# Attention scores from rounded operands: two single-pass products in place of one float32 product, in a two-layer kernel

## The reference, cut to what matters

```
# first layer: NSA (selected and window branch), MoBA
s = einsum(q, k) * scale
s = s - slope[h] * (t_query - t_key)          # ALiBi
p = softmax(where(t_key <= t_query, s, NEG)); o = p @ v
# NSA, compressed branch: 31 keys, each at the centre of a block
s = einsum(q, kc) * scale - slope[h] * (t_query - cmp_center)
# second layer: forgetting attention, c = cumsum(log_sigmoid(f)) per head
s = einsum(q, k) * scale + c[query] - c[key]
p = softmax(where(t_key <= t_query, s, NEG)); o = p @ v
```

## Time and profile before

| | |
|---|---|
| Median of 3 runs | 3514.24 us |
| The profiled execution | 3515.05 us, of which its span 3513.0 us |
| PE busy in the span | 3197.4 us (91%) |
| DVE busy | 2842.7 us (81%) |
| ACT busy | 1426.1 us (41%) |
| POOL busy | 732.3 us (21%) |
| Stage att1 | 201.6 to 383.3 us |
| Stage att2 | 1945.4 to about 2058 us |

### The profile page before, as it was taken

How to read it: one execution, slowest core, us unless ns; L and a number is a source line. 1 busy time by engine, 2 the same in 40 slices (tenths; PEclk the granted TensorE clock), 3 DMA queues, 4 the chain that set the end, 5 groups by cost and what they waited for, 6 DMA issues and landing times. The chain is left out here.

```text
span 3513.0 us, 38582 instructions
## 1 busy us (share of the span) xinstructions
PE 3197.4 (91%) x13369; PEld 2158.7 (61%) x13369; DVE 2842.7 (81%) x4722; ACT 1426.1 (41%) x1756; POOL 732.3 (21%) x724
## 2 busy tenths in 40 slices
PE   7999979999999999999999999988788888888877
PEld 4878757777777777766787788544344433344432
DVE  5877679999999999967993554788888888888886
ACT  2235348888888888853233532111111111111110
POOL 0000021000000000010000100344444444444443
PEclk9999989999999999999999999999999999999999
DMA  7422279999999999973233024999999999999998
GB/s 284 163 85 103 75 253 390 407 406 404 406 405 403 407 407 403 410 275 117 96 99 117 25 85 168 403 420 421 421 414 416 408 414 410 421 419 403 421 419 345
DMA packets 251974, 1102.12 MB, mean 314 GB/s; under 512 B 21153, under 2 KB 30753, under 8 KB 185889
## 3 DMA queue, kind: packets, MB, share of 16 engines
q1 hardware_dynamic: 166397, 525.18, 39.3%
q0 software_dynamic: 79680, 558.14, 38.8%
q10 hardware_dynamic: 5760, 17.04, 1.2%
HBM read 1071.20 MB, written 33.03 MB: 314 GB/s over the span
## 5 line engine op out<-in xcount | busy, mean ns | idle before, releaser
L2061 DVE TENSOR_TENSOR moe_w_lo<-ring,moe_w_hi 128x2048 fp32r<-128x2048 f32 x384 | 860.6, 2282 | 25.1 <-ACT moe_w_hi L1909 24.0
L1909 ACT ACTIVATE moe_w_hi<-ring 128x2048 fp32r<-128x2048 f32 x380 | 720.7, 1915 | 153.4 <-DMA ring<-in_exp_w 138.4
L2850 PE MATMUL last_banks<-last_rows_b,ring 128*128 128x512 f32 x1024 | 502.5, 638 | 127.0 <-DVE ring L3050 126.7
L2850 PE MATMUL last_banks<-last_rows_a,ring 128*128 128x512 f32 x1024 | 478.4, 611 | 80.7 <-DVE ring L3050 80.4
L2942 ACT ACTIVATE last_gelu<-last_dot 128x2 f32<-128x2 f32 (+1 forms) x257 | 52.3, 203 | 1118.0 <-DVE last_dot L3047 1117.9
L2850 PEld LDWEIGHTS last_banks<-last_rows_b,ring 128*128 128x128 f32 x1024 | 197.8, 202 | 406.6 <-issue 209.5
L2850 PEld LDWEIGHTS last_banks<-last_rows_a,ring 128*128 128x128 f32 x1024 | 188.7, 193 | 324.9 <-issue 198.8
L2729 POOL DMA_INDIRECT last_rows_a<-in_peer_uv,last_ids x256 | 284.3, 1111 | 498.8 <-PE last_banks L2850 317.2
L2729 POOL DMA_INDIRECT last_rows_b<-in_peer_uv,last_ids x256 | 292.9, 1144 | 384.5 <-PE last_banks L2850 362.6
L3050 DVE TENSOR_SCALAR ring<-consts_sb,last_gelu,last_gates 128x128 f32<-128x128 f32 x512 | 161.8, 393 | 76.0 <-ACT last_gelu L2942 74.8
L1658 POOL COPY moe_col<-slots 128x1 uint32 (+1 forms) x30 | 34.8, 1159 | 856.4 <-PE moe_tp L1705 469.9
(11 more groups left out here) (583 smaller groups left out, 6334.3 us busy)
## 6 DMA issues: line engine op xcount, KB each, us to landing
ring<-in_exp_w SPq DMA_DIRECT2D x384, 1024.0 KB, 11.2
ring<-in_w_in SPq DMA_DIRECT2D x38, 1024.0 KB, 5.1
z<-in_ada_w SPq DMA_DIRECT2D x12, 1024.0 KB, 7.3
y_rows<-moe_y ACTq DMA_DIRECT2D x17, 512.0 KB, 6.8
ring<-in_ada_w SPq DMA_DIRECT2D x4, 2048.0 KB, 14.7
ring<-in_w_out SPq DMA_DIRECT2D x8, 1024.0 KB, 4.9
y_rows<-spare SPq DMA_DIRECT2D x1, 7680.0 KB
ring<-in_ada_w SPq DMA_DIRECT2D x4, 1024.0 KB, 9.7
```

What stands on the lines that cost most here:

```text
L1909: nc.scalar.activation(w_hi[:, slot, :], env.ring[:, slot, :], ACT.Copy).then_inc(hi_done, 1)
L2061: nc.vector.tensor_tensor(w_lo[:, slot, :], env.ring[:, slot, :], w_hi[:, slot, :].bitcast(F32), ALU.subtract).then_inc(lo_done, 1)
L2850: last = nc.tensor.matmul(sums(t)[:, q, :], diag[:, n % SL], slot(n)[:, D + q * W:D + (q + 1) * W], start=first, stop=final)
```

## The change

`score` works on rounded (F32R) operands. Four tiles take the place of `qt` and `kt`: `qa` holds the query's rounded value in its low 64 rows and the rest (query minus rounded query) in its high 64 rows; `ka` holds the rounded key twice; `kb` the rest of the key and one or two rows for the bias; `qb` the rounded query and the slope (or ones). The score is `qa` by `ka` over 128 rows, plus `qb` by `kb` over 65 or 66 rows, plus the mask as before. In the first layer the row of `kb` is the key's position, in the second it is minus c, rounded, and its rest. `cmp_score` multiplies `qa` in float32 by the compressed key stored twice, and its bias is now added on DVE.

```diff
             def operand(i, m):
 
-                n = base[i] + m
-                pe.wait_ge(prep, 2 * n + 2)
+                kind, u = heads[i].operands[m]
+                src, col = (zq, heads[i].q[u]) if kind == "q" else (zk, heads[i].k[u])
                 if i:
                     pe.wait_ge(tq_moved, first_move(i, m))
+                    pe.wait_ge(tq_rest, base[i] + m)
+                    pe.wait_ge(hi_twice, base[i] + m)
                 for t in range(NT):
-                    last = nc.tensor.transpose(turn_bank(i, m)[0:AUG, t * P:(t + 1) * P], rows[:, n % 4, t, :], ident)
+                    last = nc.tensor.transpose(turn_bank(i, m)[low, t * P:(t + 1) * P], src[:, t, col:col + HD], ident)
                 last.then_inc(tq_turn, 1)
...
                 i, t, u = step(g)
                 if t == 0:
                     pe.wait_ge(tq_moved, moves_before(i))
+                    pe.wait_ge(tq_rest, base[i] + len(heads[i].operands))
+                    pe.wait_ge(hi_twice, base[i] + len(heads[i].operands))
+                    if neg_c is not None:
+                        pe.wait_ge(aug_set, 1)
+                        pe.wait_ge(decay_landed[i % 2], 64 * (i // 2 + 1))
+                    else:
+                        pe.wait_ge(aug_set, 4 * NT)
+                        pe.wait_ge(aug_ok, queries(i, len(heads[i].q)))
                 end = (t + 1) * P
-                nc.tensor.matmul(sc[:, g % 2, 0:end], qt[0:AUG, q_place(i, u), t * P:end], kt[0:AUG, k_place(i, u), 0:end], start=True, stop=False)
+                nc.tensor.matmul(sc[:, g % 2, 0:end], qa[:, q_place(i, u), t * P:end], ka[:, k_place(i, u), 0:end], start=True, stop=False)
+                nc.tensor.matmul(sc[:, g % 2, 0:end], qb[0:HD + N_AUG, q_place(i, u), t * P:end], kb[0:HD + N_AUG, k_place(i, u), 0:end], start=False, stop=False)
                 nc.tensor.matmul(sc[:, g % 2, t * P:end], ident_b[:], causal_b[:], start=False, stop=True).then_inc(scored, 1)
...
             for g in range(STEPS):
                 i, n = g // UNITS, g % UNITS
+                if i + 1 < len(heads) and 2 <= n <= len(heads[i + 1].operands) + 1:
+                    operand(i + 1, n - 2)
                 turn(g)
...
-                if i + 1 < len(heads) and 1 <= n <= len(heads[i + 1].operands):
-                    operand(i + 1, n - 1)
...
                 act.wait_ge(tq_turn, first_move(i, m) + 1)
                 kind, u = heads[i].operands[m]
-                dst = qt[0:AUG, q_place(i, u)] if kind == "q" else kt[0:AUG, k_place(i, u)]
-                nc.scalar.activation(dst, turn_bank(i, m)[0:AUG, :], ACT.Copy).then_inc(tq_moved, 1)
-
+                dst = qa[low, q_place(i, u)] if kind == "q" else ka[low, k_place(i, u)]
+                nc.scalar.activation(dst, turn_bank(i, m)[low], ACT.Copy).then_inc(tq_moved, 1)
+                act.wait_ge(tq_moved, first_move(i, m) + 1)
+                twice = qb[low, q_place(i, u)] if kind == "q" else ka[high, k_place(i, u)]
+                nc.scalar.activation(twice, dst.bitcast(F32), ACT.Copy).then_inc(hi_twice, 1)
+
+            def move_act(g):
+
+                i, t, u = step(g)
+                act.wait_ge(turned, g + 1)
+                nc.scalar.activation(probt[:, g % 2, 0:(t + 1) * P], pt[:, g % 2, 0:(t + 1) * P], ACT.Copy).then_inc(moved_act, 1)
...
+            def rest(i, m):
+
+                kind, u = heads[i].operands[m]
+                dve.wait_ge(tq_moved, first_move(i, m) + 1)
+                if kind == "q":
+                    nc.vector.tensor_tensor(qa[high, q_place(i, u)], turn_bank(i, m)[low], qa[low, q_place(i, u)].bitcast(F32), ALU.subtract).then_inc(tq_rest, 1)
+                else:
+                    nc.vector.tensor_tensor(kb[low, k_place(i, u)], turn_bank(i, m)[low], ka[low, k_place(i, u)].bitcast(F32), ALU.subtract).then_inc(tq_rest, 1)
...
             for g in range(STEPS):
                 i, n = g // UNITS, g % UNITS
-                move(g)
+                if not by_act(g):
+                    move(g)
                 if g + 2 < STEPS:
                     maximum(g + 2)
+                if i + 1 < len(heads) and 2 <= n <= len(heads[i + 1].operands) + 1:
+                    rest(i + 1, n - 2)
...
+                pool.wait_ge(zero_set, 1)
+                for n in range(4):
+                    for t in range(NT):
+                        if n + t:
+                            pool.wait_ge(aug_set, NT * n + t)
+                        nc.gpsimd.tensor_scalar(kb[aug_rows, n, t * P:(t + 1) * P], env.const("iota")[aug_rows], float(t * P), None, ALU.add).then_inc(aug_set, 1)
...
-                    nc.gpsimd.tensor_copy(rows[:, n % 4, :, 0:HD], src[:, :, col:col + HD]).then_inc(prep, 1)
-                    nc.gpsimd.tensor_copy(rows[:, n % 4, :, HD:AUG], aug).then_inc(prep, 1)
+                        nc.gpsimd.tensor_scalar(qb[aug_rows, q_place(i, u), :], env.const("ones")[aug_rows, 0:1].to_broadcast([N_AUG, S]), head.slopes[u], None, ALU.mult
+                                                ).then_inc(aug_ok, 1)
...
+                sp.wait_ge(decay_hi, 1)
+                sp.wait_ge(decay_lo, 1)
+                for i, head in enumerate(heads):
+                    if i >= 2:
+                        sp.wait_ge(scored, UNITS * (i - 1))
+                    for u in range(2):
+                        for r in range(2):
+                            sp.dma_start(kb[HD + r:HD + r + 1, k_place(i, u), :].bitcast(F32), decay[head.decays[u]:head.decays[u] + 1, r, :].bitcast(F32)).then_inc(decay_landed[i % 2], 16)
```

155 lines of the change are left out of this document (96 added, 59 removed).

## The result

| | before | changed |
|---|---|---|
| three runs, us | 3513.53 to 3518.21 | 3659.35 to 3674.99 |
| median, us | 3514.24 | 3665.11 |
| profiled execution, us (span) | 3515.05 (3513.0) | 3674.99 (3673.2) |
| ratio to before, 95% interval | | 1.0421, 1.0404 to 1.0439 |

The forecast was 3545 with a range of 3521 to 3562. The direction was right; the cost is +151 us and not +30.

A forecast was written before the change was run, and what follows sets the result against it. PE, busy 13.22 of 13.22 us in a pair, was taken as the bound. The terms 25 + 1 + 0 - 2.5 + 4 + 2 = +29.5, rounded to +30 on 3515.05, gave 3545 us, range 3521 to 3562.

The forecast's parts named there:

- PE's gain: On PE in each attention head, two rounded passes per score put a pair's scores at 2.54 us, 1.84 less.
- The loop and its waits: From one operand's transposes to the next in a pair, 2.55 us; PE waits 4.1 us a head together.
- fourth wait: After a head's fourth operand, ACT's exponential stands behind rounding and second copy: 0.65 us more waiting on PE.
- 11 x 2.3: Eleven heads whose next head has four operands, each 2.3 us slower: +25 us, bounds +13 and +32.
- the NSA heads' 0: Six NSA heads before a head with one operand: 0 each, between -1.8 and +0.6; -11 to +4 in all.
- rival D: The clock falls: stage starts alone +3 us; heads a third of the time at 1.2 GHz, +20 and more, 3570; 5%.
- D's third: In the clock-falls case, attention heads running a third of the time at 1.2 GHz: +20 us and more.
- Last heads: Last head of each attention stage, with no operands to bring: -1.2 us each, -2.5 in all.
- Start of att1: First score waits for POOL's memset, 16 small instructions and one of 512: +4 us, bounds +2 and +8.
- Start of att2: First score waits for ACT's operand work and, beside it, four DMAs: +2 us, bounds +1 and +5.
- Everything else: Weight loads, zeros, later row DMAs, and memsets and copies in convolution and compressed keys: below 0.5 us.

The follow-up runs named there:

- e9: Changed kernel without rest and second copy (operand halves filled with ones), and ACT's exponential of the compressed scores one step later: 3528.4 us, ratio 1.0026.
- e2: Kernel before with float32 scores, plus the changed kernel's operand chain alone, its added results going to memory nobody reads: 3718.1 us, ratio 1.0558.
- e13: Changed kernel without the second copy on ACT (its halves filled with ones), the rest on DVE kept: 3654.2 us, ratio 1.0361.
- e1: Changed kernel with both rounded passes of each score issued twice, in both attention stages: 3624.0 us, ratio 1.0288.
- e12: Kernel before, unchanged, profiled once more: 3512.5 us.
- e11: Changed kernel with two banks, second copy on GpSimd, start on DVE, operands, rest and exponential reordered, third small ACT copy, NSA filler matmul: 3554.9 us, ratio 1.0095.
- e6: Changed kernel with two operand banks in att2 and the second copy on GpSimd: 3628.5 us, ratio 1.0318.
- e7: Changed kernel with att1's position row made by DVE in 4 instructions instead of 16 on GpSimd: median 3656.9 us, no ratio given.
- e8: Changed kernel with two banks where the head before has no compressed branch, second copy on GpSimd, att1's position row on DVE: 3598.0 us, ratio 1.0235.

## Why the prediction was wrong

Step by step, as the prediction put them:

- **PE's gain, 1.84 us a head.** Right. Without waits a pair takes 11.53 us (e9) against 13.22: 1.69. Beside the rounding of weight tiles it is 12.26 against 13.51: 1.25. The passes themselves are dearer than forecast (see below; a pair's scores 3.1 us and not 2.54), and the turns ahead of them end earlier. DVE's 13.50 us in an NSA head is 13.52 in the earlier trace rows; nothing hangs on it.
- **The loop and its waits, 4.1 us a head.** Right. e2 shows them at full clock without the gain: 17.60 against 17.3. In e13 three waits stand nearly as forecast: from one operand's transposes to the next it is 2.70 and 2.93 us, forecast 2.55 and 2.9. No pair of the changed kernel ran at full clock throughout; 15.5 to 16.5 us is an estimate of it, from e13's 15.79, which lacks the forecast's fourth wait of 0.65. The rest's price (0.69, measured 0.68) and the second copy's (0.62, measured 0.63) hold.
- **The heads at 2.4 GHz (the terms 11 x 2.3 and the NSA heads' 0), and with it rival D, "the clock falls", 5%, +20.** This is the step that failed: the sum prices every head at full clock. The mechanism was named in D, with PE standing "1 us at a time in the heads", but priced as if a third of the time would be at 1.2 GHz. att2's heads spent nearly all of it there (0.50 and 0.57). e13 gives the price: 8.75 us a head (24.54 less 15.79); with the forecast's own +2.3 that makes 24.3 for a pair of 13.22 (measured 24.41). Even D's third was priced low: a third of some 300 us of heads is four heads of 24.4, some 35 us by this price (an estimate). From the first head's end to the last's, att2 costs +63.0, against six times 2.3 less 1.2 in the forecast, +13.
- **NSA heads at 0.** Wrong, in the main by the same step: 17.5 us at clock 0.90, 21.7 at 0.63, and +28.3 in seven intervals for which the forecast has some +3. A smaller part would have come at full clock too: at 1.00 such a head takes 16.8 us in e1, with its doubled passes, and 16.1 in e2, against 15.5 and the forecast's upper bound of 16.1. The wait at step 6 grew from 0.67 us before to 1.46. With it down to 0.44, and without rest and second copy (e9), the heads take 14.1 to 14.8, so there was a gain to be had.
- **Last heads, -1.2 each.** At full clock the last interval is 8.51 us against 9.50 (e9, e13): -1.0. In the changed kernel, at clock 0.87 and 0.88, it is 9.55 and 9.51, and nothing is gained.
- **Start of att1, +4.** Measured +9.4. The price of a small POOL instruction was taken near the 8-element copy (0.33 from bounds of 0.225 and 0.95) and was 0.60. The row of 512 was 1.50 and not 0.6, beyond the bound that I had drawn. The Trainium skill (GPSIMD Engine Reference, section on side-by-side cycle accounting) gives about 1.8 cycles an element at 1.2 GHz as GpSimd's best case, and for dispatch about 156 ns on VectorE, with two software hops on GpSimd where VectorE has one. For 512 elements an estimate from these two figures is 0.92 us. The trace has 1.50, for a single partition.
- **Start of att2, +2.** Right: 6.5 against 5.0 us, ended by the decay DMAs.
- **Everything else, below 0.5.** 21 us in the profiled pair, with no cause found (e12).

How deep the fall is shows in e13 and the changed kernel. At 2.4 GHz e13's pair is busy 12.2 of 15.8 us; once the clock is at 1.2, the same work fills 22.3 of 24.4, the waits shrink to 2.1 us, and yet the clock stays down. Returns were seen where the work changed: e13's last heads came back to 1.00 as the weight rounding on ACT ended, and e1 came back behind the head at 0.55. That the clock deserved more than 5% could be read from the forecast's own loop: it takes PE from standing 0 of 13.22 us to standing 4.1 of 15.5, in eleven heads, and the one stretch behind a rest of PE that it looked at, shows 0.64. The Trainium skill (TensorE: Matmul & The Clock Gate, section on PSUM-queue depth-cycling) describes it: a kernel whose PE idles briefly between groups of matmuls, often enough that the clock oscillates, with throughput lost although the single matmul at full clock is no slower. The forecast cited that page for weight loads and passed over this section; by it, waits in every step were the thing to price first. The traces agree in that heads full of short waits lose the clock; in the changed kernel's att2 it stayed down nearly all the time, at 0.50 and 0.57 a head.

## What to carry to other kernels

When a change makes TensorE's work smaller and puts a wait of a microsecond into each step, price the step at both clock levels before anything else: a pair here cost 15.8 us at one (e13) and 24.4 to 24.5 at the other. Read the granted clock beside the busy share, since a PE at 1.2 GHz looks like a bound. And where an engine's work shrinks, look for the waits that it used to cover (the compressed exponential at step 6): moving one ACT instruction gave back 23 to 29 us, most of what the whole gain on PE is worth (20 x 1.69).

## What the runs showed of the hardware

- Doubling the score passes made the kernel 41 us faster, and one 512-column matmul of no use ahead of each att2 operand 34 us. The clock held in att2 in both (1.00 in every head between the first and the last).
- Waits of 0.28, 0.68 and 0.20 us within 3 us were followed by 1.2 GHz (e11), while 3.3 us of waiting in a head of 18.2 were not (e1). The length of the waits alone does not tell whether the clock falls.
- A GpSimd copy of 64 x 512 from SBUF to SBUF takes 0.61 us in the median (e6), but `tensor_scalar` instructions on a single partition stand 0.60 apart for 128 elements, each waiting for the one before, and take 1.50 for 512. DVE made the same position row in 4 instructions within 3.1 us (e7), 2.2 in e8.
- Of a rounded score's two passes the first takes longer (e9, 512 keys: 0.31 and 0.24 us, 0.55 against 0.87 for float32; 256 keys: 0.20 and 0.12), where single passes stand 0.23 apart. The turns ahead of it end earlier, and the pair gains 1.69 all the same.

```profile
249.49 0.36 PE L922 MATMUL att_sc<-att_ka,att_qa 128*128 128x256 f32 x1
249.69 0.28 PE L923 MATMUL att_sc<-att_kb,att_qb 65*128 65x256 f32 x1
249.81 0.23 PE L924 MATMUL att_sc<-att_causal_b,att_ident_b 128*128 128x128 bf16 x1
...
254.13 0.47 PE L922 MATMUL att_sc<-att_ka,att_qa 128*128 128x512 f32 x1
254.44 0.40 PE L923 MATMUL att_sc<-att_kb,att_qb 65*128 65x512 f32 x1
254.68 0.23 PE L924 MATMUL att_sc<-att_causal_b,att_ident_b 128*128 128x128 bf16 x1
```
